# Modulation blocks: one in each norm turn and eleven among the pool chunks, evacuated by VectorE in the turns

## The reference

```
ada = silu(cond) @ w_ada[l] + b_ada[l]          # w_ada: 2 x 1024 x 6144, float32
sh1, sc1, g1, sh2, sc2, g2 = split(ada, 6)
u = layer_norm(x) * (1 + sc1) + sh1
m = even_mixer(u) or odd_mixer(u)               # layer 0: attention and mean pools, layer 1: gated conv and Fourier
x = layer_norm(ALPHA * x + g1 * (m @ w_out[l])) * ln_g[l, 0] + ln_b[l, 0]
u = layer_norm(x) * (1 + sc2) + sh2
x = layer_norm(ALPHA * x + g2 * conv_ffn(u)) * ln_g[l, 1] + ln_b[l, 1]
```

## Time and profile before

| | us |
|---|---|
| median of 3 runs | 2867.09 |
| lowest, highest | 2864.09, 2867.21 |
| the profiled execution | 2863.49 |
| its span, first to last instruction | 2861.5 |

### The profile page before, as it was taken

The page is one execution under the profiler, slowest core; times in us unless marked ns, Lnnn a source line. Parts: engine busy times, 40 slices in busy tenths (PEclk is TensorE's granted clock), DMA queues, the critical chain, the costliest instruction groups (busy, mean ns, idle before and its releaser), DMA issues.

```text
span 2861.5 us, 36198 instructions
## 1 busy us (share of the span) xinstructions
PE 2686.0 (94%) x13884; PEld 2379.0 (83%) x13884; DVE 1535.2 (54%) x2148; ACT 926.0 (32%) x1411; POOL 408.9 (14%) x218
## 2 busy tenths in 40 slices
PE   5698799999899999999998799999899999999997
PEld 1377577768899999999997799978899999999996
DVE  0316588866655555555557533346555555555557
ACT  1721377755422222221224621125422222222223
POOL 0005177734100000000005200014000000000002
PEclk6899899999999999999999899999999999999999
DMA  9950100022311111111111212122311111111112
GB/s 320 349 191 11 61 1 1 1 75 89 133 45 44 44 37 44 33 41 37 44 45 59 72 53 74 48 100 74 133 45 44 44 44 39 41 38 36 39 35 81
DMA packets 170558, 196.08 MB, mean 69 GB/s; under 512 B 6665, under 2 KB 124917, under 8 KB 170479
## 3 DMA queue, kind: packets, MB, share of 16 engines
q1 hardware_dynamic: 169748, 194.33, 20.5%
q10 hardware_dynamic: 731, 0.67, 0.1%
HBM read 175.64 MB, written 19.33 MB: 68 GB/s over the span
## 4 chain that ended last, share of the span: by engine, by line
PE 80%; DVE 7%; ACT 5%; POOL 3%; issue 2%; DMA 2%; ACTq 1%; SPq 0%; POOLq 0%; DVEq 0%
PE ps L1988 47%; PE ps L2208 18%; PE ps L1955 5%; POOL p_low L790 2%; PE ps L1938 2%; DMA ada_w<-in_w_ada 1%; DVE small L1516 1%; ACT ln_u L930 1%; DVE stats L1380 1%; PE ps L2141 1%; ACT p_exp L1057 1%; ACT p_top L846 1%; PE ps L2040 1%; PE ps L2098 1%; DVE acc L1629 1%
## 5 line engine op out<-in xcount | busy, mean ns | idle before, releaser
L1988 PE MATMUL ps<-act_b,uw 128*128 128x384 f32 x4608 | 807.3, 337 | 7.9 <-DVE act_b L1346 6.4
L1988 PEld LDWEIGHTS ps<-act_b,uw 128*128 128x128 f32 x4608 | 803.5, 189 | 9.7 <-DVE act_b L1346 7.0
L1988 PE MATMUL ps<-act_a,uw 128*128 128x384 f32 x3456 | 610.1, 338 | 9.0 <-DVE act_a L1346 7.6
L1988 PEld LDWEIGHTS ps<-act_a,uw 128*128 128x128 f32 x3456 | 604.5, 190 | 15.9 <-DVE act_a L1346 8.1
L2208 PE MATMUL ps<-dw,hh 128*128 128x512 f32 x2112 | 503.7, 398 | 9.5 <-DVE acc L1629 9.5
L2208 PEld LDWEIGHTS ps<-dw,hh 128*128 128x128 f32 x2112 | 399.0, 189 | 109.3 <-DVE acc L1629 10.2
L1629 DVE TENSOR_TENSOR acc<-acc,ps 128x512 f32<-128x512 f32 x360 | 245.8, 686 | 216.4 <-PE ps L2208 216.4
L846 ACT ACTIVATE fa<-ps 128x384 f32<-128x384 f32 (+2 forms) x176 | 67.3, 410 | 838.7 <-PE ps L1988 838.7
L1590 DVE TENSOR_SCALAR ft<-fa,fgrp 128x1153 f32<-128x1153 f32 x44 | 38.7, 880 | 299.0 <-ACT fa L846 284.2
L1346 DVE TENSOR_TENSOR uw<-raw_u,uw 128x1024 fp32r<-128x1024 f32 x112 | 136.6, 1221 | 116.4 <-ACT uw L846 112.2
L790 POOL TENSOR_TENSOR p_low<-p_exp,p_top 128x1536 fp32r<-128x1536 f32 (+1 forms) x50 | 170.6, 3412 | 94.3 <-ACT p_top L846 94.1
(11 more groups left out here) (206 smaller groups left out, 3129.3 us busy)
## 6 DMA issues: line engine op xcount, KB each, us to landing
raw_u<-in_w_up SPq DMA_DIRECT2D x88, 512.0 KB, 4.0
ada_w<-in_w_ada SPq DMA_DIRECT2D x72, 512.0 KB, 6.8
raw_d<-in_w_down SPq DMA_DIRECT2D x44, 512.0 KB, 3.7
late_w<-in_w_ada SPq DMA_DIRECT2D x24, 512.0 KB, 5.2
raw_u<-in_w_in_odd SPq DMA_DIRECT2D x20, 512.0 KB, 3.9
ln_y<-in_x_all SPq DMA_DIRECT2D x18, 512.0 KB, 5.5
xs<-ln_y SPq DMA_DIRECT2D x18, 512.0 KB, 2.6
acc<-xs SPq DMA_DIRECT2D x6, 1536.0 KB, 11.9
```

The lines of the kernel that those rows point to most:

```text
L1988: mm = pe.matmul(out, uw[:, u_slot, w, k, :], src[:, k, a, c * CH:(c + 1) * CH], start=(k, w, a) == (0, 0, 0), stop=(k, w, a) == (KD - 1, ...
```

## The change

- Blocks 0 to 12 are early, 13 to 23 late (`ADA_LATE` 13). Steps 0 to 8 of the norm have one block each (4 to 12), step 9 none. `ada_half` maps block numbers to other columns accordingly.
- In the turns VectorE copies the block out of PSUM, at the end of its step (`ada_evac`); ScalarE only issues the two row stores at the end of its own step, once that copy is done (`ada_store`). ScalarE still evacuates blocks 0 to 3 (`top_evac`) and the late ones.
- A late block stands after each pool chunk from (0,1) on: block 13 after (0,1), 14 after (0,2), and so on to 23 after (3,2). `late_w` has six buffers, two of them over `ln_y`, free once the last `ln_z` is written.
- SyncE's order of the late loads, the bias rows and the loads of `wq` and `wkv` is written anew. Two of the four `wkv` conversions on ScalarE move ahead of group 3's copies. VectorE's second `cols_of` moves behind the splits of `wkv`.
- The projection's pool mixing waits for `cols_done` instead of the last evacuation; SyncE waits for all stores before it reads the gate rows.

```diff
 def ada_half(m):
-    if m < 6:
+    if m < 4:
         return 0, m
-    if m < 10:
-        return 1, m - 6
-    return (0, m - 4) if m < 16 else (1, m - 12)
+    if m < 7:
+        return 1, m - 4
+    if m < 13:
+        return 0, m - 3
+    return (1, 3) if m == 13 else (0, m - 4) if m < 16 else (1, m - 12)

 def ada_steps(kind):
-    return {s: [4 + 2 * s, 5 + 2 * s] if s < 3 else [7 + s] if s < 9 else [16, 17] for s in range(10)}
+    return {s: [4 + s] for s in range(9)} if kind == "in" else {}

-ADA_LATE = 18
-LATE_CHUNKS = {(0, 2): 18, (1, 1): 19, (2, 0): 20, (2, 2): 21, (3, 1): 22}
-LATE_SLOTS = 4
+ADA_LATE = 13
+ADA_ALL = 24
+LATE_CHUNKS = {(m // 3, m % 3): ADA_LATE - 1 + m for m in range(1, 12)}
+LATE_SLOTS = 6
...
@@ SyncE, late_units
-                    sp.wait_ge(ada_used, a + 1 + ADA_SLOTS - LATE_SLOTS)
-                    sp.dma_start(late_w[:, slot, :, :], w[u][:, :, half * 512:half * 512 + 512]).then_inc(late_ld[slot], 16)
+                    a = 4 * (m - ADA_LATE) + u
+                    if a >= LATE_SLOTS:
+                        sp.wait_ge(ada_used, ADA_SLOTS + 4 * ADA_LATE + a - LATE_SLOTS + 1)
+                    elif a == 4:
+                        sp.wait_ge(z_rdy, NT)
+                    sp.dma_start(late_w[a % LATE_SLOTS][:], w[u][:, :, half * 512:half * 512 + 512]).then_inc(late_ld[a % LATE_SLOTS], 16)
...
@@ SyncE, order of the loads
-            for m in range(4, 6):
-                ada_units(m)
+            ada_units(4)
...
-            late_units(18)
-            bias_rows(range(2, 4), 16)
...
+            late_units(13)
+            bias_rows(range(2, 4), ADA_LATE)
+            wq_unit(2)
+            wq_unit(3)
+            for m in (14, 15, 16):
+                late_units(m)
+            wq_unit(4)
+            wq_unit(5)
+            late_units(17)
+            late_units(18)
+            bias_rows(range(4, 6), ADA_LATE + 1)
+            late_units(19)
+            wq_unit(6)
+            wq_unit(7)
+            late_units(20)
+            late_units(21)
+            wkv_unit(0)
+            wkv_unit(1)
+            late_units(22)
+            late_units(23)
+            wkv_unit(2)
+            wkv_unit(3)
...
@@ ScalarE, end of a norm step
-                act.wait_ge(ada_st[slot], 32 * (turn + 1) if i is None else i * 32 + 32 * (turn + 1))
-                copy(ada_row[:, slot, :], ps[:, 3 + m % 3, :]).then_inc(ada_bank, 1)
                 act.wait_ge(ada_bank, m + 4 if i is None else i * 3 + (m + 4))
                 for c in range(2):
                     act.dma_start(ada[l, c::2, bass.ds(col, 512)], ada_row[c::32, slot, :]).then_inc(ada_st[slot], 16)
...
@@ VectorE, end of a norm step
+            def ada_evac(m, i=None):
+                slot, turn, used = (m - ADA_TOP) % 3, (m - ADA_TOP) // 3, ADA_SLOTS + 4 * m + 4
+                v.wait_ge(ada_used, used if i is None else i * 12 + used)
+                if turn:
+                    v.wait_ge(ada_st[slot], 32 * turn if i is None else i * 32 + 32 * turn)
+                v.tensor_copy(ada_row[:, slot, :], ps[:, 3 + m % 3, :]).then_inc(ada_bank, 1)
...
@@ TensorE
             ln_turns("in", lambda c: pool_chunk(0, c))
+            late_block(LATE_CHUNKS[0, 1])
             for n in range(U_POOL, U_FFN0):
                 for c in range(0 if n else 2, NCH):
                     pool_chunk(n, c)
                     if (n, c) in LATE_CHUNKS:
-                        late_block(LATE_CHUNKS[n, c], 4 if n >= 2 else None)
+                        late_block(LATE_CHUNKS[n, c])
                 if n in (1, 3):
-                    pe.wait_ge(ada_bank, 3 + (20 if n == 1 else 23))
+                    pe.wait_ge(ada_bank, 3 + (18 if n == 1 else ADA_ALL))
                     cols_mm(range(n + 1, n + 3))
-            late_block(23, 6)
```

More of the change, by code:

```diff
@@ L209, in build @@
         ada_w = at("ada_w", [P, ADA_SLOTS, 2, 512], F32, off_b)
-        late_w = at("late_w", [P, LATE_SLOTS, 2, 512], F32, off_b + 55680)
+        late_w = [at(f"late_w{i}", [P, 2, 512], F32, off_b + 55680 + 4096 * i if i < 4 else off_s + 4096 * (i - 3)) for i in range(LATE_SLOTS)]
         late_row = [at(f"late_row{i}", [P, 512], F32, off_s + 2048 * i) for i in range(2)]
@@ L366, in ada_stored @@
             for s in range(3):
[L367 to L370, removed]
+                eng.wait_ge(ada_st[s], 32 * len(range(s, ADA_LATE - ADA_TOP, 3)))
+            for s in range(2):
+                if n > ADA_LATE + s:
+                    eng.wait_ge(late_st[s], 32 * ((n - ADA_LATE - s + 1) // 2))
         class Step:
@@ L570, in _, with wq_unit, wkv_unit @@
             ln_loads("in", t["x_all"])
-            late_units(18)
-            bias_rows(range(2, 4), 16)
-            for k in range(2, KD):
+            def wq_unit(k):
                 d_unit(D_QKV + k, t["w_in_even"][0][k * P:(k + 1) * P, 0:AW], AW)
[L575 to L585, removed]
+            def wkv_unit(k):
                 n = D_QKV + KD + k
@@ L656, in _ @@
             sp.wait_ge(pv_done, TURNS)
+            ada_stored(sp, ADA_ALL)
             gate_rows(0)
@@ L678, in _ @@
             u_unit(U_CONV, w_conv[:, :, 0:P])
-            bias_rows(range(6, 8), 24)
+            bias_rows(range(6, 8), ADA_ALL)
             for k in range(4):
@@ L897, in u_hi_at @@
                 copy(uw[:, slot, 0, :, :], raw_u[:, slot, :, :]).then_inc(u_hi, 1)
-            for m in range(4):
-                ada_evac(m)
+            for m in range(ADA_TOP):
+                top_evac(m)
             for n in range(2):
@@ L970, in _, with wkv_hi @@
             ln_act("in", act_a)
+            def wkv_hi(k):
+                n = D_QKV + KD + k
+                act.wait_ge(d_loaded[n % 2], 16 * (n // 2 + 1))
+                copy(wkv[:, 2 * k:2 * k + 2, 0, :], raw_d[:, n % 2, 0:512].rearrange("p (a n) -> p a n", a=2)).then_inc(d_hi, 1)
             act.wait_ge(pp_zero, 1)
@@ L986, in _ @@
                         late_evac(LATE_CHUNKS[n, c])
-            for k in range(KD // 2):
-                n = D_QKV + KD + k
-                act.wait_ge(d_loaded[n % 2], 16 * (n // 2 + 1))
-                copy(wkv[:, 2 * k:2 * k + 2, 0, :], raw_d[:, n % 2, 0:512].rearrange("p (a n) -> p a n", a=2)).then_inc(d_hi, 1)
+            wkv_hi(2)
+            wkv_hi(3)
             def heads(ap):
@@ L1444, in _ @@
                     d_lo_at(D_QKV + k, k % 2, wq[:, k, 1, :], wq[:, k, 0, :], AW)
-                if n in (1, 3):
-                    cols_of(range(n + 1, n + 3))
+                if n == 1:
+                    cols_of(range(2, 4))
             for k in range(KD // 2):
```

49 lines of the change are left out of this document (24 added, 25 removed).

## The result

The changed kernel takes **2877.26 us** (median of 7 runs, 2874.56 to 2881.70) against 2867.09: a ratio of 1.0039, with a 95% interval of 1.0030 to 1.0049. Of seven runs of before one took 3397.41 us; the ratio leaves it out. The change is slower by about 10 us, where 1.4 were forecast. The profiled execution took 2874.56 us, its span is 2873.0 us, 11.5 above that of before.

The account below looks back on a forecast made before the run. TensorE, busy for 94% of the span, was taken to bound the kernel. Terms -8.0 + 7.4 + 3.4 + 1.6 + 1.4 - 3.9 + 1.6 - 2 = +1.5 us gave 2868.5 us, 8-in-10 range 2858 to 2878.

Parts of the forecast that it names:

- norm turns (to the end of chunk (0,2)): Norm turns: first turn starts 13.2 us sooner, seven turns each 1.47 longer, last split at 136.9 instead of 144.84: -8.0 us.
- four more late blocks: Pool chunks on TensorE: ten late blocks from chunk (0,2) on instead of six, 1.85 us each: +7.4 us.
- wait at block 14: First late block after chunk (0,2): TensorE waits for its loads, complete at about 147.1: +3.4 us (0 to 6).
- slow chunk behind it: Pool chunk behind block 14 runs at the lower clock after TensorE's wait: +1.6 us (0 to 2).
- hardly any: Late blocks after the first one behind chunk (0,2): hardly any further TensorE wait for late_w; no term in the sum.
- waits of the columns for the eviction: Pool stage: twice the column matmuls stand right behind a late block and wait about 0.7 us each for its evacuation: +1.4.
- end of stage: End of pool stage: block 23 and VectorE's wkv split move ahead of the columns and are hidden by them: -3.9 us.
- projection: Projection to q, k, v: cold start +1.6, less overlap of GpSimd's pool sums with VectorE's rope pieces -2 us.
- The rival of loads that fall behind: Late blocks wait in sequence if loads run below 358 GB/s; 2875 us at 325 GB/s; 0.27, shared with cold clocks at waits.
- the turn: Norm turn: VectorE's copy behind its split delays ScalarE's store issues and next ln_u, 7.80 to 9.27 us, 1.47 longer.
- The rival of a turn that is not longer: Norm turns: ScalarE's wait hides VectorE's copy, seven turns stay at 7.80 us; 2858 us; chance 0.10.
- the slow start of the projection: Projection starts right behind the columns, with block 23 no longer warming the clock: +1.6 us (0 to 2).

Follow-up runs that it names:

- experiment 1: Changed kernel with block 14's loads asked for ahead of the bias rows and wq pieces: 2869.2 us, ratio to before 1.0016.
- experiment 5: Changed kernel with wkv units 0 and 1 asked for behind block 22's units on SyncE's queue: 2873.93 us, ratio to before 1.0025.
- experiment 3: Changed kernel with VectorE's copy of the block ahead of its split in the norm turn: 2860.98 us, ratio to before 0.9989.
- experiment 12: Changed kernel with wq units 2 and 3 asked for behind block 14's units instead of ahead of them: 2871.61 us, ratio to before 1.0027.
- experiment 6: Changed kernel with columns ahead of blocks 16 and 20, and GpSimd's pool sums waiting for block 23's matmuls: 2882.04 us, ratio to before 1.0050.
- experiment 11: Kernel before the change, with GpSimd's pool sums also waiting for block 23's eviction: 2863.6 us, ratio to before 0.9995.
- experiment 2: Changed kernel with ScalarE again copying the block out of PSUM in the norm turns, block spread kept: 2866.01 us, ratio to before 1.0003.
- experiment 7: Changed kernel in which SyncE asks for block 15's units only when all of block 14's have landed: 2879.2 us, ratio to before 1.0038.
- experiment 8: Changed kernel with the edits of experiments 1, 3, 5 and 6 together: 2856.56 us, ratio to before 0.9963.
- experiment 9: Kernel of experiment 8 with wq units 6 and 7 converted earlier and wkv loaded and converted earlier: 2853.39 us, ratio to before 0.9957.
- experiment 10: Kernel of experiment 9 with chunk (0,0) behind the transposes of its norm turn on TensorE: 2850.92 us, ratio to before 0.9955.

## Why the prediction was wrong

It forecast no change, by terms that cancel; the terms of gain held and those of loss were too small. The wide range, 2858 to 2878 us, holds the 2877.26 by less than a microsecond, and that is luck: its upper end was set for the rival whose mechanism did not come. (The bounds of the forecast's own terms add up to 2876, not to the 2873 that it gives.) Up to the first projection matmul, from the timelines of TensorE (the parts of after are differences of starts, less the 1.85 us of a block and the 4.37 of a warm chunk):

| Term | Forecast, us | Measured, us |
|---|---|---|
| norm turns (to the end of chunk (0,2)) | -8.0 | -8.6 |
| four more late blocks | +7.4 | +7.4 |
| wait at block 14 | +3.4 (0 to 6) | +7.2 |
| slow chunk behind it | +1.6 | +0.75 |
| waits at blocks 20 to 22 | "hardly any" | +2.8 |
| waits of the columns for the eviction | +1.4 | +1.4 |
| first columns at the lower clock | none | +1.5 |
| end of stage | -3.9 | -3.6 |
| sum with small differences (0.7) | +1.9 | +9.6 |
| projection | -0.4 | -0.8 |

- **The step that failed is the wait at block 14.** "Units follow each other by about 1.3", so that "block 14 is complete at about 147.1": it was complete at 149.4. The 1.3 came from two units of before in a short burst. Here four units follow 0.52 MB of wq in a queue at rest; the experiment with wq behind gives 146.2 for the second half, so without wq the forecast was right to a microsecond, and wq ahead, worth 2.5 us, is what it left out of the value ("6 if the wq loads push in", its upper bound, was 1.2 too low). Of the 3.8 us that are missing 2.3 are this landing, 0.7 TensorE's earlier arrival, and 0.9 the second half, which ran at the lower clock (1.94 us, granted 0.50 in 148 to 150) behind its wait. Asking for block 14 earlier takes the whole wait away and leaves 1.71 us of it to block 15 (experiment 1).
- **"Hardly any later"** failed at blocks 20 to 22. I had costed the moved wkv loads at nothing, as 392 GB/s leaves room; the rate wasn't it. SyncE stood in order at wkv unit 0 (197.1 to 200.7), until VectorE had split wq unit 6 behind ScalarE's conversion at the start of group 3, with block 22's units queued behind it (experiment 5). This covers block 22's 1.7 of the 2.8 us; what held blocks 20 and 21 for the other 1.0 stays open. The rival of loads that fall behind, whose 2875 us come near the result, thus had the right sign and the wrong mechanism: in the busiest stretches the loads move 374 to 407 GB/s, above its 358, and the mean over 143 to 215 is 307, with the queue's stands in it. The Trainium skill's 358 GB/s per core ("SBUF — State Buffer", section "A bandwidth-pool intuition that's wrong") is below what these stretches move.
- **The columns' clock** was missing. I costed the wait for the eviction and not that the columns, or what stands behind them, run slow: 5.23 us for the first ones, at a mean granted clock of 0.71 in 171 to 177, and 6.08 for the chunk behind. What sets it stays open. Behind the same block and wait the columns took from 3.73 us (the last ones of experiment 3) to 6.21 (the first ones of experiment 12); right behind a chunk they took 3.73 to 4.92 (experiments 6 and 11), and the slow stretch then fell on what followed (3.56 us for a block).
- **Right** was the turn: 1.53 us longer for 1.47, since ScalarE's stores, and its next ln_u, wait for a copy that stands behind the split. The copy took 0.68 us, the estimate from "VectorE: DVE Perf Modes" of the Trainium skill (section "The TRN2 errata") was 0.66. Experiments 2 and 3 show both cause and remedy. The rival of a turn that is not longer thus needed only another order of VectorE's two instructions.
- **Right** were also the end of the stage and the projection. GpSimd's later start gives 2.1 to 2.5 us (2 forecast), shown by itself in experiment 11, with tile 1 free and tile 2 paying; the slow start of the projection takes some 1.7 back (1.6 forecast), as its first six pairs of matmuls take 3.9 us instead of 2.2.

## What to carry to other kernels

When work moves from a stage that is full into one that has room, cost each of its loads by what stands ahead of it in its queue and by what the queue's engine itself waits for, in order, and not by the mean rate of the stage: here 0.52 MB ahead of one block and one wait ahead of another cost 2.5 and 1.1 us (experiments 12 and 5) of a change whose gain was 8. When an instruction moves to another engine, look for a wait of that engine that can cover it: behind the split the copy lengthened every turn by 1.5 us, ahead of it it was free. And what removes a cover exposes the next wait: ask what the removed work hid before taking the saving.

## What the runs showed of the hardware

- In the changed kernel the queue of large loads that starts from rest moves 287, 322 and 352 GB/s in 140 to 146, and up to 407 later (169 to 171); in experiment 1 another start from rest, at 137.26, gave 398 in 140 to 142. What stands ahead of a load delays it (0.52 MB: 2.5 us), what is asked for behind it hardly does (0.6 us at most, experiment 7).
- In every run the 32 column matmuls of this stage, or what stands right behind them, run slow. Where the columns keep the full clock (3.73 us), what follows does not: a block takes 3.3 to 3.6 us instead of 1.92 (experiments 6, 8, 9 and 10), at a granted clock of 0.53 in 166 to 169 of experiment 6. A wait of 0.72 us ahead of them does not decide it (3.73 us behind it in experiments 2, 3 and 7). No run has the columns behind a block without a wait.
- Whether GpSimd's sums begin 5 us ahead of the projection or with it makes 2.1 us of the projection's length (94.24 or 92.14), with the same work on both engines (experiment 11).
